# Branch products of the first two layers as split products, with changed instruction orders on ScalarE and VectorE

## The reference, cut to what matters

```python
h = rmsnorm(x, mix_norm_g[l])
u = h @ w_in                       # queries, keys, ... and mgate of 4 x 1024 columns
# four mixers of width 256: retention, SSD, GLA, mLSTM
y_ret = head_rmsnorm(o, ret_norm_g) * silu(rg)          # the others alike
ybr   = stack([y_ret, y_ssd, y_gla, y_ml], axis=2)
gates = sigmoid(mgate.reshape(bsz, seq, 4, 1024))
merged = sum(gates * einsum('bsnv,nvd->bsnd', ybr, w_branch), axis=2)
x = x + merged @ w_out
h = rmsnorm(x, ffn_norm_g[l])
x = x + (swiglu(h, w1, w3, w2) if l == 0 else moe_ffn(h, router_w, w1, w3, w2))
```

## Time and profile before

| | us |
|---|---|
| median of 3 runs | 2626.9 (2621.12 to 2627.77) |
| the profiled execution | 2627.28 |
| its span, first to last instruction | 2625.4 |
| busy: PE | 2451.9 (93%) |
| busy: DVE | 1670.7 (64%) |
| busy: ACT | 1359.6 (52%) |
| busy: POOL | 366.9 (14%) |
| weights read | 547 MB, 209 GB/s |

### The profile page before, as it was taken

One profiled execution on the slowest core, in us unless ns is written; L12 is line 12 of the kernel. 1 busy time (PEld: TensorE's weight loads), 2 busy tenths in 40 slices (PEclk: granted clock), 3 DMA queues, 4 the chain that ended last, 5 costly groups with the idle time before them and its releaser, 6 DMA issues.

```text
span 2625.4 us, 31712 instructions
## 1 busy us (share of the span) xinstructions
PE 2451.9 (93%) x11717; PEld 1976.2 (75%) x11717; DVE 1670.7 (64%) x2387; ACT 1359.6 (52%) x1721; POOL 366.9 (14%) x209
## 2 busy tenths in 40 slices
PE   7998899999987899999999999989989988998998
PEld 6876688798765677787787787767768866776886
DVE  5755655466555789889898898843455553345554
ACT  4543254445422578778787787725434432543443
POOL 2254000003530000000000000025510002550000
PEclk9998999999988899999999999999999998999999
DMA  7523375344331999999999999744465524446550
GB/s 218 192 98 130 119 261 184 108 149 150 111 129 61 319 334 353 318 331 354 317 344 341 320 361 320 265 134 158 147 211 198 187 80 134 154 152 208 192 192 33
DMA packets 381700, 549.36 MB, mean 209 GB/s; under 512 B 27221, under 2 KB 283593, under 8 KB 381465
## 3 DMA queue, kind: packets, MB, share of 16 engines
q1 hardware_dynamic: 377392, 535.82, 59.9%
q0 software_dynamic: 3920, 11.58, 1.6%
q10 hardware_dynamic: 288, 0.59, 0.1%
HBM read 546.91 MB, written 1.05 MB: 209 GB/s over the span
## 4 chain that ended last, share of the span: by engine, by line
PE 80%; DVE 10%; ACT 3%; DMA 3%; issue 2%; POOL 1%; DVEq 0%; ACTq 0%; SPq 0%
PE mb L903 14%; PE mb L905 13%; PE mb L904 13%; PE pb L903 8%; PE pb L905 8%; PE pb L904 8%; DMA ring<-in_w_in 3%; PE pb L1320 2%; DVE w_lo L2497 2%; PE pb L881 2%; PE pb L886 2%; PE pb L1023 1%; ACT w_hi L1612 1%; PE mb L1154 1%; POOL w_lo L755 1%
## 5 line engine op out<-in xcount | busy, mean ns | idle before, releaser
L2497 DVE TENSOR_TENSOR w_lo<-ring,w_hi 128x1024 fp32r<-128x1024 f32 x444 | 534.1, 1222 | 221.8 <-ACT w_hi L1612 173.4
L1612 ACT ACTIVATE w_hi<-ring 128x1024 fp32r<-128x1024 f32 x324 | 332.5, 1054 | 359.8 <-DMA ring<-in_w_in 204.1
L903 PE MATMUL mb<-w_hi,hT_hi 128*128 128x512 f32 x1232 | 494.9, 402 | 13.6 <-DVE w_lo L2497 8.3
L905 PE MATMUL mb<-w_lo,hT_hi 128*128 128x512 f32 x1232 | 482.2, 391 | 0.0
L755 POOL TENSOR_TENSOR w_lo<-ring,w_hi 128x1024 fp32r<-128x1024 f32 x136 | 330.1, 2454 | 517.3 <-ACT w_hi L1612 517.0
L903 PE MATMUL pb<-w_hi,hT_hi 128*128 128x512 f32 (+1 forms) x896 | 345.2, 385 | 11.3 <-DVE low_rows L2497 7.6
L2497 DVE TENSOR_TENSOR w_lo<-down_w,w_hi 128x1024 fp32r<-128x1024 f32 x242 | 293.8, 1222 | 88.2 <-ACT w_hi L1612 79.3
L905 PE MATMUL pb<-w_lo,hT_hi 128*128 128x512 f32 (+1 forms) x896 | 336.6, 376 | 0.0
L904 PE MATMUL pb<-w_hi,low_rows 128*128 128x512 f32 (+1 forms) x896 | 336.3, 375 | 0.0
L903 PEld LDWEIGHTS mb<-w_hi,hT_hi 128*128 128x128 f32 x1232 | 232.2, 189 | 72.1 <-DVE w_lo L2497 25.1
L1759 ACT ACTIVATE w_hi<-ring 128x1024 fp32r<-128x1024 f32 x256 | 268.1, 1057 | 19.9 <-PE mb L905 17.3
(11 more groups left out here) (452 smaller groups left out, 3714.9 us busy)
## 6 DMA issues: line engine op xcount, KB each, us to landing
ring<-in_moe_w SPq DMA_DIRECT2D x128, 1024.0 KB, 7.8
ring<-in_w_in SPq DMA_DIRECT2D x50, 2048.0 KB, 8.2
down_w<-in_moe_w SPq DMA_DIRECT2D x88, 1024.0 KB, 11.1
third_gu<-in_moe_w SPq DMA_DIRECT2D x48, 1024.0 KB, 9.2
down_w<-in_w_ffn_down SPq DMA_DIRECT2D x22, 1024.0 KB, 10.0
ring<-in_w_out SPq DMA_DIRECT2D x8, 2048.0 KB, 8.2
ring<-in_ffn_w SPq DMA_DIRECT2D x16, 1024.0 KB, 8.0
ring<-in_w_ffn_gate SPq DMA_DIRECT2D x16, 1024.0 KB, 5.5
```

Of the source, the lines that this page charges most:

```text
L903: mm(o, a_hi, hi, start=start, stop=False)
L905: return mm(o, a_hi, lo, start=False, stop=stop)
L1612: f(w_hi[:, m % NPIECE], src, ACT.Copy).then_inc(w_hi_ready, 1)
L2497: return tt(dst, src, hi.bitcast(F32), ALU.subtract)
```

## The change

Layers 0 and 1:

- `w_branch` becomes two pieces a branch (one for each half of the columns, 256 rows), loaded by half rows (`half_view`), in the numbering behind the gates: two behind `gate(1,1)`, two behind `gate(2,1)`, one in the middle of `gate(3,1)`, three at its end. The low parts are POOL's, which now makes M+8 to M+47; `w_out` is M+48 to M+55. The slot of a branch item is free when its last low part is made.
- merge(b) on PE makes split products. `yT` becomes `yT_hi` (ACT) and `yT_lo`, which DVE makes in `y_low`, one operation on the PSUM bank, in between its other work: before `head_norm` of branches 1 and 2, between rounds of GLA for branch 2's y, after `head_norm` of branch 3. The bank of the turned y counts as emptied by DVE's `y_low`.
- ACT's order: the copy of y comes before or right behind two branch pieces; more `high_to` in between. DVE makes `w_out`'s low parts M+48, M+49 before merge(3), M+50, M+51 behind it, ahead of the low part of `merged`, and M+52 to M+55 after that; before, four ahead of merge(3) and four after the low part of `merged`.
- `poolT` and `sguT` of layers 2 and 3 move to the memory of `u_ret`.

Elsewhere: in layer 3 `square_sums` no longer waits for both tiles of `xn`; ACT's order in `mixers2` (`high_to(M+16)` for `high_to(M+18)` before `gate(1,0)`; `high_to(M+22)` and `high_to(M+30)` go, and their pieces are made by the next `high_to`); `final_and_first` makes `xn` with one reciprocal root, and `rstd` for `x` after it; in an expert pass the low parts 1 to 3 stand between the two halves of `xg_lo`, and the four operations on `selT` and `slot_no` move from the pass's head to its end.

The diff, cut to its core:

```diff
 def split_items1():
+    whole = lambda key, count=4: [(key, q) for q in range(count)]
+    items = []
...
+    items += whole(("branch", 0), 2) + whole(("gate", 2, 0)) + whole(("gate", 2, 1)) + whole(("branch", 1), 2)
+    last = whole(("gate", 3, 1))
+    items += whole(("gate", 3, 0)) + last[:2] + [(("branch", 2), 0)] + last[2:] + [(("branch", 2), 1)] + whole(("branch", 3), 2)
+    return items + whole(("wout", 0)) + whole(("wout", 1))
...
+        def half_view(n):
+
+            return lambda s, src: ring[:, s, n * PIECE:(n + 1) * PIECE].rearrange("p (k n) -> p k n", k=2)
...
+                    w = a["w_branch"][L, BR_ORDER[b]]
+                    for h in range(2):
+                        loads.append((half_view(2 * n + h), w[:, h * 512:(h + 1) * 512].rearrange("(k p) n -> p k n", p=P)))
...
-                low_parts(MIX[L] + HEAD_PIECES + 8, MIX[L] + HEAD_PIECES + 40)
+                low_parts(MIX[L] + HEAD_PIECES + 8, MIX[L] + HEAD_PIECES + 48)
...
             def merge(L, b, hs=range(2)):
-                at = 2 * D * (b == 3)
-                w = weights((L, "branch", b))[:, at:at + 2 * D].rearrange("p (k n) -> p k n", k=2)
-                acted(BK[L], ("yturn", b))
+                pe.wait_ge(yT_split, NBR * L + b + 1)
                 for h in hs:
+                    m = PC.of[(L, "branch", b, h)]
+                    pe.wait_ge(*low_done(m))
                     for i in range(T):
+                        it = slice(i * P, (i + 1) * P)
                         bank = open_bank(BK[L], ("merge", b, h, i))
                         for kk in range(2):
-                            ins = mm(bank[:], yT[:, b % 2, kk, i * P:(i + 1) * P], w[:, kk, h * 512:(h + 1) * 512],
-                                     start=kk == 0, stop=kk == 1)
+                            ins = split_product(bank[:], yT_hi[:, kk, it], yT_lo[:, kk, it], m, slice(kk * 512, (kk + 1) * 512),
+                                                kk == 0, kk == 1)
                         ins.then_inc(filled, 1)
...
-            def square_sums(n, ready):
-
-                if n:
+            def square_sums(n, ready, by_tile=False):
+
+                if n and not by_tile:
                     act.wait_ge(xn_ready, T * n)
...
                 ins.then_inc(qkt_ready, 1)
+                high_to(M + 24)
+                yturned(L, 0)
                 high_to(M + 26)
-                yturned(L, 0)
                 gate(L, 1, 1)
-                high_to(M + 28)
+                high_to(M + 30)
                 act.wait_ge(gla_arg, 2 * L + 1)
                 f(gla_e.rearrange("p l s -> p (l s)"), gla_e.rearrange("p l s -> p (l s)"), ACT.Exp).then_inc(gla_exp, 1)
-                high_to(M + 30)
+                high_to(M + 32)
                 gate(L, 2, 0)
                 high_to(M + 34)
                 yturned(L, 1)
+                high_to(M + 36)
                 gate(L, 2, 1)
-                high_to(M + 38)
+                high_to(M + 40)
...
                 yturned(L, 2)
+                high_to(M + 42)
                 gate(L, 3, 0)
-                high_to(M + 40)
+                high_to(M + 46)
                 gate(L, 3, 1)
-                high_to(M + 44)
+                high_to(M + 50)
                 yturned(L, 3)
...
-                high_to(M + 18)
+                high_to(M + 16)
                 gate(L, 1, 0)
...
                 merged_turned(L)
-                high_to(MIX[L] + HEAD_PIECES + 48)
+                high_to(MIX[L] + HEAD_PIECES + 56)
...
+            def y_low(L, b):
+
+                v.wait_ge(yT_hi_ready, NBR * L + b + 1)
+                low(yT_lo.rearrange("p k s -> p (k s)"), pb[BK[L].index[("yturn", b)] % 4][:],
+                    yT_hi.rearrange("p k s -> p (k s)")).then_inc(yT_split, 1)
+                v.wait_ge(yT_split, NBR * L + b + 1)
...
+                y_low(L, 0)
                 head_norm(L, 1, 3, u_ml[:, :, ML_O:ML_O + MW], False)
                 merge(L, 0)
...
+                y_low(L, 1)
                 head_norm(L, 2, 0, u_ret[:, :, 768:1024], False)
                 merge(L, 1)
...
+                y_low(L, 2)
                 gla_put_levels(L, 3)
...
                 head_norm(L, 3, 2, u_gla[:, :, 4 + MW:], False)
+                y_low(L, 3)
                 merge(L, 2, (1,))
-                low_range(MIX[L] + HEAD_PIECES + 40, MIX[L] + HEAD_PIECES + 44)
+                low_range(M + 48, M + 50)
                 merge(L, 3)
+                low_range(M + 50, M + 52)
...
                 v.wait_ge(squares, 5 * T)
                 link(ts(r_in, ssq, 1.0 / D, EPS, ALU.mult, ALU.add))
-                rsqrt(rstd, r_in)
-                link(tt(r_in, rstd, rstd, ALU.mult))
+                link(ts(m_out, r_in, EPS, None, ALU.mult))
                 v.wait_ge(squares, 6 * T)
...
+                rsqrt(rstd_out, m_out)
...
                     for half in range(2):
-                        low_parts(half, 1 + 2 * half)
                         v.wait_ge(xg_hi_ready, 2 * t + half + 1)
                         low(xg_lo[:, 4 * half:4 * half + 4], mb[2 + half][:].rearrange("p (k s) -> p k s", k=4),
                             xg_hi[:, 4 * half:4 * half + 4]).then_inc(xg_ready, 1)
-                    v.wait_ge(scatter_mm, 2 * t + 2)
...
+                        if half == 0:
+                            low_parts(0, 3)
...
+                    places_back()
                     v.wait_ge(e_used, t * ALL_PIECES + ALL_PIECES + NPIECE)
```

More of the change, by code:

```diff
@@ L222, in __init__, with add @@
         self.n, self.maker, self.of = 0, [], {}
-    def add(self, key, count, maker):
-        for q in range(count):
-            self.of[key + (q,)] = self.n
-            self.maker.append(maker)
-            self.n += 1
+    def add(self, key, maker):
+        self.of[key] = self.n
+        self.maker.append(maker)
+        self.n += 1
     def nth(self, m):
@@ L234, with __init__ @@
 class Banks:
-    def __init__(self, jobs, fill_base, act_base, dve_base, layer):
+    def __init__(self, jobs, fill_base, act_base, dve_base, layer, split_base=0):
         self.jobs = jobs
-        self.by = ["dve" if j[0] in ("merge", "wout") or (j[0] == "turn" and 4 <= j[1] < 8) else "act" for j in jobs]
+        self.by = ["dve" if j[0] in ("merge", "wout") or (j[0] == "turn" and 4 <= j[1] < 8) else (
+            "split" if j[0] == "yturn" and len(j) == 2 else "act") for j in jobs]
+        self.split0 = split_base
         n_act, n_dve = self.by.count("act"), self.by.count("dve")
@@ L252, in emptied @@
         who = self.by[n]
+        if who == "split":
+            return who, self.split0 + job[1] + 1
         return who, (self.act0 if who == "act" else self.dve0) + self.by[:n + 1].count(who)
@@ L411, in build @@
         pool_w = soft[:].rearrange("p t n -> p (t n)")[:, 0:P].rearrange("p (a d) -> p a d", a=2)
-        poolT, sguT, attT = yT[:, 0], yT[:, 1], ch_in[:, 0:4]
+        poolT, sguT, attT = u_ret[:, :, 512:768], u_ret[:, :, 768:1024], ch_in[:, 0:4]
         y_sgu = u_gla[:, :, 0:MW]
@@ L491, in build @@
             MIX[L] = PC.n
-            for key in (split_items1() if L < 2 else split_items2()):
-                head = L < 2 and key[0] == "proj" and key[1] < 6
-                PC.add((L,) + key, CHUNK_PIECES[key[1]] if head else 4, "dve" if key[0] in ("proj", "wout") and L < 2 or key[0] == "wout" else "pool")
+            for key, q in (split_items1() if L < 2 else split_items2()):
+                by_dve = key[0] == "wout" or (key[0] == "proj" and L < 2)
+                PC.add((L,) + key + (q,), "dve" if by_dve else "pool")
             if L != 1:
@@ L497, in build @@
                 FFN[u] = PC.n
[L498 removed]
+                for q in range(ALL_PIECES):
+                    PC.add(("ffn", u, q), "dve")
         def low_done(m):
@@ L506, in build @@
         for key, m in PC.of.items():
-            if key[0] != "ffn" and key[:-1] + (key[-1] + 1,) not in PC.of:
+            if key[1] == "branch":
+                closing[m] = BK[key[0]].filled(("merge",) + key[2:] + (T - 1,))
+            elif key[0] != "ffn" and key[:-1] + (key[-1] + 1,) not in PC.of:
                 L, job = key[0], key[1:-1]
@@ L564, in split_item @@
             count = width * KD // PIECE
-            first = PC.of[(L,) + key + (0,)]
+            m_of = [PC.of[(L,) + key + (q,)] for q in range(count)]
             loads = []
@@ L569, in split_item @@
                 loads.append((cols_view(width, at), w[:, c0:c0 + cols[2 * n + 1]].rearrange("(k p) n -> p k n", p=P)))
-            add_item((L,) + key, s, loads, low_done(first + count - 1))
+            add_item((L,) + key, s, loads, low_done(m_of[-1]))
             for q in range(count):
-                source[first + q] = (ring[:, s, q * PIECE:(q + 1) * PIECE], find[(L,) + key] if q == 0 else None)
+                source[m_of[q]] = (ring[:, s, q * PIECE:(q + 1) * PIECE], find[(L,) + key] if q == 0 else None)
         def ffn_items(u, L, w1, w3, w2):
```

(16 more changed lines are left out.)

58 lines of the change are left out of this document (25 added, 33 removed).

## The result

The changed kernel takes 2644.1 us (median of 4 runs, 2642.9 to 2646.1) against 2624.6 us (2621.1 to 2627.8): ratio 1.0075, 95% interval 1.0058 to 1.0093, 15 to 24 us slower. Its profiled execution took 2642.91 us, with a span of 2641.1.

The account below looks back on a forecast made before the run. PE, 80% of the chain, bounds the kernel. 2627.3 + 39.7 (layers 0 and 1) - 12 (experts) - 14 (layers 2 and 3) - 1 (squares) = 2640, less 2 for layer 3 gaps: 2638 us; range 2608 to 2651.

Parts of the forecast that it names:

- part 1: Branch products, layers 0 and 1: split products save 12 us of PE time, on the path only at merge(1).
- part 3: Layers 0 and 1: eight more POOL pieces a layer delay head_norm; layer 0 12.2 us behind, layer 1 14.5.
- Rival A: Layers 0 and 1: POOL holds up wide DVE operations alone; 2616 us; chance 0.20.
- Rival B: Layers 0 and 1: a DVE operation meeting POOL's ready pieces waits for the whole burst; 2646 us; chance 0.11.
- part 4: Stage end, layers 0 and 1: head_norm of branch 3 later by 2.0 us, w_out's start by 4.7 us.
- part 5: Experts' eight passes: the new order cuts PE's waits for w_lo and xg_lo; -12 us, bounds -10 and -14.
- part 6: Layers 2 and 3: ACT's new order cuts PE's waits at gates and merges; -14 us, bounds -9 and -16.
- the squares by tile: Layer 3: squares of the first tile start before the second tile is written; -1 us.
- for the layer 3 gaps that a load would end anyway: Layer 3: a final 2 us taken off the sum, from 2640 to 2638 us.
- Rival C: Layers 0 and 1: POOL's bursts are looser, half the delay of part 3 goes; 2627 us; chance 0.20.
- rival D: Experts and layers 2 and 3: part 5 and part 6 bring half; 2651 us; chance 0.06.

Follow-up runs that it names:

- experiment 4: The changed kernel with each POOL low part as two instructions of 128x512 instead of one of 128x1024; 2631.8 us, ratio 1.0018.
- experiment 5: The changed kernel with ACT making the high parts of M+50 and M+51 right behind the copy of branch 3's y; 2632.1 us, ratio 1.0017.
- experiment 1: The kernel before with only the changed orders (square_sums, mixers2, final_and_first, experts' pass), no split branch products; 2601.1 us, ratio 0.9899.
- experiment 2: The changed kernel with those orders put back, so only the split branch products of layers 0 and 1 stay; 2662.2 us, ratio 1.0136.
- experiment 6: The changed kernel with POOL waiting for y of branches 1 and 2, and ACT's earlier high parts at the stage's end; 2605.1 us, ratio 0.9911.
- experiment 7: The kernel of experiment 6 with POOL's low parts as two instructions of half the size; 2586.7 us, ratio 0.9844.
- experiment 9: The changed kernel with POOL making 8 of 1024 columns of the branch pieces' low parts, the rest left out; 2607.4 us, ratio 0.9925.

## Why the prediction was right, point by point

The forecast was 2638 us, slower; measured 2644. The mechanism and its place held, and so did the size in layers 0 and 1 (39.7 us forecast, 39.9 measured), though two terms in it missed by 2.3 and 2.6 us a layer and cancelled. That the whole came so near is in part luck. The prediction starts from the profiled execution of before (2627.3 us) and so forecast +10.7; the profiles differ by 15.6 us, of which 4.3 are the late start, so by 11.4 without it. In this the experts, layer 2 and the stretch to layer 3's first gate gave 6.7 us more than their terms and layer 3 gave 7.4 less than its own. The medians differ by 19.5 us; where the other 4 lie no profile shows.

**PE's saving (part 1) and its worth.** The term was 8 x 1.5 = 12 us. That PE's total busy time fell by 11.7 is a coincidence: the branch products alone lower it by 7.8 us (2444.1), the orders alone by 4.4 (2447.5). At the full clock a merge went from 7.11 to 5.76 us, 1.35 each, so the term should have been 10.8 us. All ten stretches of merges in layers 0 and 1 together fell from 64.9 to 50.6 us, 4.4 of which were merge(1)'s low clock in before (9.82 and 8.80 us against 7.11). None of it is seen in the time of the changed kernel.

**POOL's bursts (part 3).** Forecast were six pieces in a row, seven operations done by their end, and an idle PE of nearly 10 us; measured were six pieces, six held-up operations and the reduction, 9.18 us. gate(2,0) was put at 200.3 and gate(3,0) at 246.2; with the 4.3 us of the late start taken off they stood at 200.0 and 244.5. The next GLA round came 9.9 us later, not 12.2: between its pieces M+35 and M+36 lay 0.34 us and not 1.4, and it ended earlier for that, and the low clock behind each gap cost 1.3 us (six matmuls in 2.69 us, against 1.37 at the usual pace), not 2. Operations on 128 x 8 took 2.26 to 2.33 us in the burst, the wide one 2.49. The rule of the Trainium skill on the shared port (page SBUF — State Buffer, section "SBUF: two separate sides") blocks the second comer for the whole instruction and makes no exception for small ones. The trace agrees. Rival A fell with the small operations' times. Rival B fell in these bursts with the operation that gets in behind each piece, which experiment 4 confirmed at half the size; at the start of layer 2 its behaviour, known from the 8.02 us of the earlier trace rows, stayed (9.85 us in after).

**The end of the stage (part 4).** Forecast 2.0 + 4.7 - 0.2 = 6.5 us in layer 0; measured 9.1 (19.0 less 9.9). This is the term that was too small, and it made up for the 2.3 us above. The wait before w_out grew from 1.90 us to 6.42, by 4.5 where 4.7 was worked out. merge(3) ended 2.8 us later (1.8 forecast). What the sum had left out is the clock while PE turns `merged`: behind a wait of the same length it took 1.94 us in before and 3.57 in after (319.70 above), 1.6 us more.

```profile
302.66 1.94 PE L859 MATMUL pb<-cst,merged 128*128 128x128 f32 x16 [3.22 <-DVE merged L2070]
```

Why the clock fell earlier in after is open. Experiment 5 gave 12 us back over two layers where 10 were expected.

**The experts (part 5).** Forecast -12, measured -15.7. The wait for w_lo is gone in seven passes, as forecast, and so is the one for xg_lo (5.1 us in the earlier trace rows); in the first pass 3.2 us for xg_lo have become 2.6 for w_lo, 0.6 less, where 0.7 was forecast. PE's waits in after, 900 to 1730 us:

```profile
PE mb L1268 <- DVE gates L2652: 5.0, 1, 5.0
PE mb L925 <- DVE w_lo L2533: 2.6, 1, 2.6
```

From one pass's wait for u_z to the next's it is 101.06 us on average, where it was 103.13: a pass was 2.07 us shorter, and 1.84 was worked out. Of the 3.7 us that the term was short, 1.6 are this and 1.6 the rounding down from 13.6 to 12.

**Layers 2 and 3 (part 6).** In layer 2 the whole change gave what was forecast or a little more (with final_and_first, -10.7 up to the squares of layer 3), though the orders alone gave 4.3 (experiments 1 and 2). Of the 2.8 us around layer 3's first norm only about 1 is the squares by tile, as forecast: in experiment 2, which lacks that edit, the same stretch had moved by 1.8 us. Layer 3's gates are the one step that failed. By the starts on PE, merge(0) came 1.6 us earlier and merge(1) is 4.6 us better off behind the vanished wait, as worked out (1.5 and 4.2). Between them 4.7 us were lost, and 1.7 more behind the gates, so that the layer ended 0.3 us better by the table. PE of before and of after, DVE and POOL of after in layer 3:

```profile
2314.01 2.89 PE L1356 MATMUL mb<-u_ml,ch_in 128*128 128x64 f32 x24
```
```profile
2329.56 4.77 PE L1379 MATMUL mb<-u_ml,ch_in 128*128 128x64 f32 x24 [1.96 <-DVE ch_in L2435]
```
```profile
2316.50 2.62 DVE L2416 TENSOR_TENSOR merged<-merged,gates 128x512 f32<-128x512 f32 x1
...
2325.46 2.06 DVE L2416 TENSOR_TENSOR merged<-merged,gates 128x512 f32<-128x512 f32 x1
2327.55 1.95 DVE L2435 COPY ch_in<-mb 128x384 f32<-128x384 f32 x4
```
```profile
2316.22 10.75 POOL L777 TENSOR_TENSOR w_lo<-ring,w_hi 128x1024 fp32r<-128x1024 f32 x4 [9.61 <-ACT w_hi L1635]
```

Four adds that read SBUF twice wait for POOL's burst, 2.0 to 2.6 us each; PE waits 2.0 us for DVE's copies behind them and drops to the low clock. The adds met a burst in before too (1.10, 2.01, 2.01 and 2.05 us), but the copies were then ready when PE came to them. The earlier merge leaves PE without that slack, and the first add takes 1.5 us more. It is the mechanism of part 3, and the forecast had looked for it in layers 0 and 1 only. With POOL's instructions halved and nothing else changed (experiment 4) PE does not wait there. The orders alone lost time in the same way in layer 2 (PE waits 1.6 us for ch_in).

The 2 us taken off the sum "for the layer 3 gaps that a load would end anyway" have the wrong sign. A load that ends a gap anyway makes the gain smaller and the time longer, so by its own words the sum is 2642 and not 2638.

**What was not foreseen.** Each execution starts differently: the third item of weights landed 3.4 us later in after's profile than in before's. Such a scatter of up to 4.5 us can hide in every comparison of single profiles. Rival C (bursts looser than drawn) and rival D did not come about.

## What to carry to other kernels

Before work is given to an idle GpSimd, ask which VectorE operations run at that moment on SBUF. In these traces each of them with two inputs there, or with one and a scalar, however small, waited for the GpSimd instruction under way, so a chain of small dependent operations is the worst neighbour. If the work must be there, let GpSimd wait for the end of the chain or cut its instructions in two; both, with the earlier high parts at the stage's end, turned a change that lost 0.75% into one that gains 1.6%. And split a diff of several hunks by experiment: here half of it was worth 1% and was hidden by the other half.

## What the runs showed of the hardware that was not expected

- A 128x1024 subtraction on GpSimd took 2.45 us whole, 2.72 in two instructions, 3.10 in four (waits included), and 0.20 to 0.25 us at 128x8.
- Behind a wait of PE of 3.9 us the first matmul took 0.77 us, at the low clock; behind one of 1.6 us at the same place, in a kernel that differs in POOL's halves alone, it took 0.47 us, and the clock fell 1.2 us later (experiments 6 and 7).
- A GpSimd instruction on SBUF held up VectorE operations on SBUF of 128x8 and of 128x512 numbers alike. It did not hold up a reduction of 128x512 (0.69 us from 187.56 in after), nor products with one input in PSUM: in experiment 7 four of them took 2.87 us from 189.00 with POOL busy from 189.05 on.
- In most bursts one held-up VectorE operation got in behind each GpSimd instruction. At the start of layer 2 one waited for the whole burst: 8.02 us in before, 9.85 in after, 11.57 with quarters, but not in experiments 4 and 9.
